# Paged attention of a decoder step: page loads two pages at a time, two low parts on other engines, products over three bank pairs

## The chip, the core and the metric

The kernel runs on one core of one Trainium2 chip. The metric is the device time of one execution in microseconds. The engines in the text: PE is TensorE, DVE is VectorE, ACT is ScalarE, POOL is GpSimd, and SP (SPq in rows) is the sync engine, which here computes nothing: it reads page numbers into registers and issues DMAs. Each engine runs its own instructions in program order; semaphores tie the engines together.

## What is computed

One layer of a hybrid decoder: a half SwiGLU block, one input projection, a convolution branch and a latent attention branch, a gated merge, and a second half SwiGLU block, for 512 prompt tokens and 8 sequences of 8 sample tokens. The change touches only the attention of the 8 sample sequences. Each has 2048 past positions, in 16 pages of 128 rows that a page table names:

```
def one_seq(args):
    q_s, ckv_new, kpe_new, pages = args
    ckv = concat([cache_ckv[pages].reshape(past, 256), ckv_new])
    kpe = concat([cache_kpe[pages].reshape(past, 32), kpe_new])
    k = rmsnorm([einsum('lc,chd->lhd', ckv, w_uk) | kpe], k_head_norm)
    s = einsum('qhd,khd->hqk', q_s, k) * SCALE        # masked
    p = softmax(s)
    return einsum('qhc,chd->qhd', einsum('hqk,kc->qhc', p, ckv), w_uv)
```

Products of full precision are made of three cheaper ones: each operand is split into a high part (a rounded copy) and a low part (the operand minus its high part), and high*high, low*high and high*low are summed.

## The kernel before

Every engine has one hand-written program; the order in it is the order of the work. The sample attention is a stage of 8 sequences (s = 0 to 7) of 16 pages (t), taken in 8 pairs of pages (pp). `sequences` gives the frame on each engine: s = 0 alone, a hardware loop of two sequences a turn, and the last three written out; SP has s = 0 and 1 alone and then its own loop of three turns over s = 2 to 7.

For a pair of pages: SP loads two transposed pages into `c_ring` (8 slots, so four pairs); ACT rounds them to `cT_hi` (`pages_hi`), DVE subtracts to `cT_lo` (`pages_lo`, line 2466), both two deep. PE multiplies each page with the queries and the key weights (line 1861: 12 products of 288 columns), page t into PSUM banks 2 and 3 or 4 and 5 by turns (`page_banks`). ACT copies the scores to `s_buf` and squares the rest into `sq`; DVE sums the squares to `page_ss`. At every fourth page PE adds the rotary scores from `kpeT`.

The softmax of sequence r runs inside sequence r + 1 (`soft_act`, `soft_dve`, `soft_pe`). It needs `kpe_sq`, which POOL makes from all 16 pages of `c_nat`, the rows of the same pages as they lie (line 964). ACT makes the exponentials `p_two`; POOL makes their low part (line 945) and that of the value rows `c_lo` (line 937), and PE multiplies both in two batches of four pairs, before page 12 and before page 15 (lines 1781, 1782), then sums the denominator (line 1791) and folds (line 1796).

SP's part is `load_pages`, four times a sequence: it reads four page numbers from SBUF into registers (`page_of`, line 726, one TENSOR_LOAD each), and with these registers issues four DMAs to `c_ring` (line 731), four to `kpeT` (line 742) and four to `c_nat` (line 737). Three waits stand before them, for `ct_lo` (the ring's slots are free), `pe_scored` and `pages_used`. Behind the last of these on SP stand the loads of the merge weights `w_rawbuf` (line 618), and ACT's program holds their rounding (`split_hi`, line 461) between pairs 4 and 5 of s = 7.

Of the kernel before, what the change touches and what calls it, by code (L numbers as in the profile page):

```python
# [14 lines left out]
F32 = mybir.dt.float32  # L15
# [5 lines left out]
ds = bass.ds  # L21
# [72 lines left out]
def layer(nc, x_t, cols_in, pages_t, pages_in, pages_k, state_conv, page_table, w, const, out):  # L94

    ctx = ExitStack()
    with ctx:
# [14 lines left out]
        def sem(name):  # L112
            return ctx.enter_context(nc.semaphore(name))
# [197 lines left out]
        split_made = sem("split_made")  # L311
# [14 lines left out]
        nat_in = [[sem(f"nat_in{b}{g}") for g in range(NP // 4)] for b in range(2)]  # L326
        ring_in = [sem(f"ring_in{g}") for g in range(2)]
# [194 lines left out]
        SPLITS = PAIRS + 2  # L522
        HIGHS = PAIRS + 2
        LATE_AT = 11
# [9 lines left out]
        def pair_made(r, j):  # L534

            return r * SPLITS + (EARLY_PAIRS + 1 if j < EARLY_PAIRS else j + 3)

# [10 lines left out]
        PEB = 6  # L548

# [24 lines left out]
        def page_banks(t):  # L574

            return 2 + 2 * (t % 2)
# [19 lines left out]
        def _(sp):  # L596
# [131 lines left out]
            def load_ring(g, found):  # L728

                for u, page in enumerate(found):  # L730
                    sp.dma_start(c_ring[:, (4 * g + u + RING // 2) % RING, :], pages_t[ds(page, 1), :, :].rearrange("a p c -> (a p) c"))\  # L731
                        .then_inc(ring_in[g % 2], 16)

            def load_rows(b, g, found):

                for u, page in enumerate(found):
                    sp.dma_start(c_nat[:, b, 4 * g + u, :], pages_in[ds(page, 1), :, :].rearrange("a p c -> (a p) c")).then_inc(nat_in[b][g], 16)  # L737

            def load_kpe(g, found):

                for u, page in enumerate(found):
                    sp.dma_start(kpeT[u * DR:(u + 1) * DR, g % 2, :], pages_k[ds(page, 1), :, :].rearrange("a d t -> (a d) t")).then_inc(kpe_in[g % 2], 16)  # L742
# [12 lines left out]

            sp.wait_ge(rows_done, 2 * NT + PT_TILES)
            found = [page_of(0, u) for u in range(4)]
            load_ring(0, found)
            load_kpe(0, found)
            sp.wait_ge(prep_q, 1)  # L760
            load_rows(0, 0, found)
            for g in (1, 2):
                load_rows(0, g, [page_of(0, 4 * g + u) for u in range(4)])
            sp.wait_ge(prep_tr, 2)
            sp.wait_ge(uk_split, 1)
            found = [page_of(0, 4 + u) for u in range(4)]
            load_ring(1, found)
            load_kpe(1, found)
            load_rows(0, 3, [page_of(0, 12 + u) for u in range(4)])
            for g in (2, 3):  # L770
                found = [page_of(0, 4 * g + u) for u in range(4)]
                sp.wait_ge(ct_lo, 2 * g - 2)
                load_ring(g, found)
                sp.wait_ge(pe_scored, g - 1)
                load_kpe(g, found)
            sp.wait_ge(prep_mm, 2)
            load_pages(1, 1)
# [38 lines left out]
        def _(pool):  # L816
# [124 lines left out]
            def probabilities_low(r, b, half):  # L941

                t = slice(half * NP // 2, (half + 1) * NP // 2)
                pool.wait_ge(p_done, exp_made(r, half))
                ins = pool.tensor_tensor(p_two[:, t, 1, :], s_buf[:, b, t, :], p_two[:, t, 0, :].bitcast(F32), ALU.subtract)
                if half:
                    ins = pool.tensor_tensor(p_two[0:TS, NP, 1, :], s_buf[0:TS, b, NP, :], p_two[0:TS, NP, 0, :].bitcast(F32), ALU.subtract)
                ins.then_inc(split_made, 1)

            def squares(s, b, uses, prev, nxt):  # L950

                if prev and stacked(s):
                    for j in range(EARLY_PAIRS):
                        split_pair(s - 1, 1 - b, j)
                    for half in range(2):
                        probabilities_low(s - 1, 1 - b, half)
                    for j in range(EARLY_PAIRS, PAIRS):
                        split_pair(s - 1, 1 - b, j)
# [19 lines left out]
        def _(act):  # L978
# [316 lines left out]
            def pages_hi(s, pp):  # L1295

                act.wait_ge(ring_in[pp // 2 % 2], (s * 2 + (pp // 4 + 1)) * 64)
# [30 lines left out]
            def pair_high(r, b, j, uses):  # L1328

                act.wait_ge(nat_in[b][j // 2], uses * 64)  # L1330
                act.wait_ge(pages_used, r * PAIRS + (j + 1))
                act.activation(c_hi[j % EARLY_PAIRS][:, :, 0:KL], c_nat[:, b, 2 * j:2 * j + 2, 0:KL], ACT.Copy).then_inc(p_done, 1)
# [99 lines left out]
        def _(pe):  # L1432
# [333 lines left out]
            def soft_pe(r, b):  # L1766
# [8 lines left out]
                if stacked(r + 1):  # L1775
                    for j in range(PAIRS):
# [51 lines left out]
            def pe_seq(s, b, uses, prev, nxt):  # L1828
                soft = soft_pe(s - 1, 1 - b) if prev else None
                for pp in range(NP // 2):  # L1830
# [5 lines left out]
                    for u in range(2):  # L1836
# [5 lines left out]
                        if not (isinstance(s, int) and s == 0 and t < 2):  # L1842
                            pe.wait_ge(page_sq, s * NP + (t - 1))
# [4 lines left out]
                        if prev and stacked(s):  # L1848
                            for _ in range({12: 4, 15: 4}.get(t, 0)):
                                next(soft)  # L1850
                        cols = slice(SQ * b, SQ * b + KQ)
                        for k in range(2):
                            c = (2 * u + k) * P
                            hi, lo = cT_hi[:, pp % 2, c:c + P], cT_lo[:, pp % 2, c:c + P]
                            if prev and k == 1 and t in ((7, 8, 15) if stacked(s) else (7, 8)):
# [79 lines left out]
        def _(dve):  # L1935
# [527 lines left out]
            def pages_lo(s, pp):  # L2463

                dve.wait_ge(ct_hi, s * PAIRS + (pp + 1))
                dve.tensor_tensor(cT_lo[:, pp % 2, :], ring_pair(pp), cT_hi[:, pp % 2, :].bitcast(F32), ALU.subtract).then_inc(ct_lo, 1)  # L2466

# [17 lines left out]
            pages_lo(0, 0)  # L2485
# [11 lines left out]
            def soft_dve(r, b):  # L2497
# [33 lines left out]
                if stacked(r + 1):  # L2531
                    dve.wait_ge(lat_mm, r + 1)
                    dve.tensor_copy(o_lat[:, :], ps[:, 7, 0:PAGE_COLS]).then_inc(soft_step, 1)
                    dve.wait_ge(p_summed, r + 1)
# [67 lines left out]

            def dve_seq(s, b, uses, prev, nxt):
                soft = soft_dve(s - 1, 1 - b) if prev else None
                taps = iter(range(PER))
                for pp in range(NP // 2):
                    if pp + 1 < NP // 2 or nxt:
                        pages_lo(s, pp + 1)
# [34 lines left out]
                    for u in range(2):  # L2643
# [3 lines left out]
                        if prev and stacked(s) and t == NP - 2:  # L2647
                            next(soft)
# [128 lines left out]
```

## Time and profile before

| | us |
|---|---|
| median of three runs (1536.82 to 1539.36) | 1537.03 |
| the profiled execution | 1533.52 |
| its span, first to last instruction | 1531.5 |
| granted TensorE clock, mean share of full | 0.994 |

The sample stage lies at about 706 to 1018 us of the span; before it are the first half block, the projections and the prompt attention, after it the merge and the second half block. The profile shows for each engine when its instructions ran, what ended each idle stretch, and the chain of work that ended last. Rows of SP have the time of issue of a DMA, not of its transfer.

### The profile page before, as it was taken

The page shows a single profiled execution, that of the slowest core. Times are in us where ns is not written, and L with a number is a line of the kernel's source. Part 1 is how long each engine was busy: PE and PEld are TensorE (multiplying, and loading weights), DVE is VectorE, ACT ScalarE, POOL GpSimd, SP SyncE. Part 2 cuts the span into 40 slices and gives each one's busy share as a digit, 9 for nine tenths or more (in the row PEclk, how much of TensorE's full clock was granted, in tenths as well). Part 3 has the DMA queues.
Part 4 walks back from the last instruction along what each step waited for, and adds up shares of the span by engine and source line. Part 5 has one row for each costly group of instructions (what it writes and reads, how often), then busy time and mean ns, then how long its engine had stood idle before and what let it go on. Part 6 is the DMA issues. An engine that isn't in the chain of part 4 may idle for free.

```text
span 1531.5 us, 31143 instructions
## 1 busy us (share of the span) xinstructions
PE 1491.3 (97%) x10771; PEld 1434.9 (94%) x10771; DVE 1067.9 (70%) x1738; ACT 655.5 (43%) x1215; POOL 454.3 (30%) x463
## 2 busy tenths in 40 slices
PE   8999999999999999999999888999999999999999
PEld 8999999999999999588888888888999999999999
DVE  7999898421269975865888788854759998985000
ACT  6444445322221242464666666642434444445111
POOL 4000002454465744320344333223551000005432
PEclk9999999999999999999999999999999999999999
DMA  6233234222333651003444443432222332332322
GB/s 176 70 103 103 82 97 116 78 83 75 82 83 100 83 116 47 13 4 99 129 127 129 124 125 111 128 106 72 83 83 56 109 97 85 106 92 81 91 77 82
DMA packets 245460, 141.69 MB, mean 93 GB/s; under 512 B 22705, under 2 KB 242290, under 8 KB 245362
## 3 DMA queue, kind: packets, MB, share of 16 engines
q1 hardware_dynamic: 244498, 139.97, 33.1%
q8 instruction: 54, 0.88, 0.2%
q10 hardware_dynamic: 864, 0.48, 0.1%
q14 instruction: 44, 0.36, 0.1%
HBM read 136.82 MB, written 3.58 MB: 92 GB/s over the span
## 4 chain that ended last, share of the span: by engine, by line
PE 52%; issue 24%; SPq 11%; POOL 7%; DVE 3%; ACT 1%; DMA 1%; POOLq 0%; DVEq 0%; ACTq 0%
PE ps L493 28%; PE ps L1522 14%; POOL w_lobuf L468 7%; SPq L726 3%; SPq L731 3%; SPq L742 3%; SPq L737 2%; PE ps L1861 2%; PE ps L1647 1%; PE ps L1701 1%; PE ps L1676 1%; PE ps L479 1%; PE ps L1691 1%; DMA w_rawbuf<-in_ffn_w_gu 1%; DVE cT_lo L2466 1%
## 5 line engine op out<-in xcount | busy, mean ns | idle before, releaser
L468 POOL TENSOR_TENSOR w_lobuf<-w_rawbuf,w_hibuf 128x256 fp32r<-128x256 f32 (+1 forms) x328 | 316.4, 996 | 801.4 <-ACT w_hibuf L461 801.3
L1522 PE MATMUL ps<-xs,w 128*128 128x288 f32 x3192 | 427.7, 296 | 0.8 <-DVE w L1984 0.8
L1522 PEld LDWEIGHTS ps<-xs,w 128*128 128x128 f32 x3192 | 426.8, 188 | 1.5 <-issue 1.5
L461 ACT ACTIVATE w_hibuf<-w_rawbuf 128x1024 fp32r<-128x1024 f32 (+1 forms) x89 | 104.4, 1173 | 353.3 <-PE ps L493 332.9
L2192 DVE SCALAR_TENSOR_TENSOR xT<-ps,xT 128x576 f32<-128x576 f32 x23 | 17.4, 756 | 202.4 <-PE ps L493 202.4
L1984 DVE TENSOR_TENSOR w<-w_raw,w 128x512 fp32r<-128x512 f32 x228 | 154.0, 690 | 0.3 <-ACT w L1029 0.2
L493 PE MATMUL ps<-a_hi,w_lobuf 128*128 128x288 f32 x682 | 147.5, 297 | 0.0
L493 PE MATMUL ps<-a_hi,w_hibuf 128*128 128x288 f32 x682 | 147.2, 296 | 0.0
L493 PE MATMUL ps<-x_hi,w_hibuf 128*128 128x288 f32 x656 | 142.2, 298 | 4.1 <-POOL w_lobuf L468 2.9
L493 PE MATMUL ps<-a_lo,w_hibuf 128*128 128x288 f32 x682 | 145.5, 294 | 0.0
L493 PE MATMUL ps<-x_lo,w_hibuf 128*128 128x288 f32 x656 | 140.8, 296 | 0.0
L493 PE MATMUL ps<-x_hi,w_lobuf 128*128 128x288 f32 x656 | 140.7, 296 | 0.0
L1029 ACT ACTIVATE w<-w_raw 128x512 fp32r<-128x512 f32 x228 | 132.2, 624 | 5.7 <-DVE w_raw L1978 2.4
L1861 PE MATMUL ps<-kq_hi,cT_hi 128*128 128x288 f32 x512 | 119.6, 316 | 14.7 <-DVE cT_lo L2466 9.3
L2215 DVE SCALAR_TENSOR_TENSOR y<-ext,cols,y 128x512 f32<-128x512 f32 x120 | 110.6, 922 | 4.1 <-DVE y L2215 1.4
L1861 PE MATMUL ps<-kq_hi,cT_lo 128*128 128x288 f32 x512 | 111.3, 299 | 0.0
L1861 PE MATMUL ps<-kq_lo,cT_hi 128*128 128x288 f32 x512 | 111.3, 299 | 0.0
L493 PEld LDWEIGHTS ps<-x_hi,w_hibuf 128*128 128x128 f32 x656 | 105.4, 188 | 5.8 <-POOL w_lobuf L468 4.1
L493 PEld LDWEIGHTS ps<-a_hi,w_hibuf 128*128 128x128 f32 x682 | 110.2, 189 | 0.0
L493 PEld LDWEIGHTS ps<-a_lo,w_hibuf 128*128 128x128 f32 x682 | 109.3, 188 | 0.0
L493 PEld LDWEIGHTS ps<-a_hi,w_lobuf 128*128 128x128 f32 x682 | 109.0, 188 | 0.0
L1861 PEld LDWEIGHTS ps<-kq_hi,cT_hi 128*128 128x128 f32 x512 | 84.1, 194 | 25.3 <-DVE cT_lo L2466 10.4
(335 smaller groups left out, 2602.6 us busy)
## 6 DMA issues: line engine op xcount, KB each, us to landing
w_raw<-in_ffn_w_gu SPq DMA_DIRECT2D x76, 256.0 KB, 2.9
up_rows<-in_ffn_w_gu SPq DMA_DIRECT2D x72, 256.0 KB, 3.2
c_nat<-in_pages_in SPq DMA_DIRECT2D x128, 144.0 KB, 2.2
c_ring<-in_pages_t SPq DMA_DIRECT2D x128, 128.0 KB, 2.1
w_rawbuf<-in_w_in SPq DMA_DIRECT2D x58, 256.0 KB, 3.2
w_rawbuf<-in_ffn_w_down SPq DMA_DIRECT2D x32, 384.0 KB, 4.0
w_rawbuf<-in_ffn_w_down SPq DMA_DIRECT2D x32, 320.0 KB, 3.4
w_rawbuf<-in_ffn_w_gu SPq DMA_DIRECT2D x24, 256.0 KB, 3.4
```

Source lines behind the costliest of these rows:

```text
L461: act.activation(w_hibuf[:, r % HIS, 0:size], w_rawbuf[:, r, 0:size], ACT.Copy).then_inc(w_hi_done, 1)
L468: ins = pool.tensor_tensor(w_lobuf[:, r, part], w_rawbuf[:, r, part], w_hibuf[:, r % HIS, part].bitcast(F32), ALU.subtract)
L493: mm = pe.matmul(ps[0:width, 2 * s + h, 0:HALF], a, b[:, k, h * HALF:(h + 1) * HALF], start=first and i == 0 and j == 0, stop=last and i = ...
L726: return sp.value_load(pages[0:1, ds(s * NP + t, 1)], min_val=0, max_val=pages_t.shape[0] - 1)
L731: sp.dma_start(c_ring[:, (4 * g + u + RING // 2) % RING, :], pages_t[ds(page, 1), :, :].rearrange("a p c -> (a p) c"))\
L737: sp.dma_start(c_nat[:, b, 4 * g + u, :], pages_in[ds(page, 1), :, :].rearrange("a p c -> (a p) c")).then_inc(nat_in[b][g], 16)
L742: sp.dma_start(kpeT[u * DR:(u + 1) * DR, g % 2, :], pages_k[ds(page, 1), :, :].rearrange("a d t -> (a d) t")).then_inc(kpe_in[g % 2], 16)
L1029: act.activation(w7[b][:, slot, 0, :], src, ACT.Copy).then_inc(w7_hi, 1)
L1522: mm = pe.matmul(ps[:, seven_bank(f, slot), 0:HALF], m, xs[:, slot, n, k, :], start=k == 0 and j == 0, stop=k == KH - 1 and j == 2)
L1861: mm = pe.matmul(ps[:, page_banks(t) + half, 0:KQ], a, m[:, half, cols], start=k == 0 and j == 0, stop=k == 1 and j == 2)
L1984: dve.tensor_tensor(w7[b][:, slot, 1, :], w7_raw[b][:, slot, 1, :], w7[b][:, slot, 0, :].bitcast(F32), ALU.subtract).then_inc(w7_lo, 1)
L2215: dve.scalar_tensor_tensor(dst, src, cw, dst, op0=ALU.mult, op1=ALU.add).then_inc(conv_p_step, 1)
```

## The change

Five things change, all in the sample stage.

- **Loads.** SP's `load_pages` (four groups a sequence) becomes `load_pair` (eight). The list of page numbers is no longer shared: ring, rows and rotary keys each call `found` and read their own. The rows of pages 8 to 15 of sequence s - 1 are loaded among the first four ring pairs of s, those of pages 0 to 7 of s among the last four; the last group of rotary keys of s - 1 comes with pair 1 of s. `ring_in` has one semaphore a ring pair, `nat_in` one a buffer, waited for at all 16 pages.
- **Low part of pages** (`pages_lo`): from DVE to POOL, except in s = 0. On POOL `kpe_sq` of s, which waits for all rows of s, stands ahead of pair 1 of s + 1.
- **Low part of probabilities**: from POOL to DVE, at pair 5.
- **Value products**: four pairs before page 11 and four inside page 14 (before: 12 and 15); the denominator before page 15, the fold after it.
- **Banks**: page products over three pairs of banks (2 and 3, 4 and 5, 0 and 1) instead of two.

SP's program, first rows of its loop: before

```order
446 L726 TENSOR_LOAD pages
447 L726 ISA x3
448 L726 TENSOR_LOAD pages
449 L726 ISA x3
450 L726 TENSOR_LOAD pages
451 L726 ISA x3
452 L726 TENSOR_LOAD pages
453 L726 ISA x2
454 L748 ISA
455 L731 ISA [waits ct_lo]
456 L731 DMA c_ring<-in_pages_t 128x256
```

and of the change (line 736 reads a page number, 744 loads the ring, 750 the rows):

```order
504 L736 TENSOR_LOAD pages
505 L736 ISA x2
506 L764 ISA
507 L744 ISA [waits ct_lo]
508 L744 DMA c_ring<-in_pages_t 128x256
509 L744 ISA
510 L744 DMA c_ring<-in_pages_t 128x256
511 L736 ISA
512 L736 TENSOR_LOAD pages
513 L736 ISA x3
514 L736 TENSOR_LOAD pages
515 L736 ISA x2
```

The body of this loop is two sequences. It holds 32 TENSOR_LOADs and 96 DMAs before, and 96 TENSOR_LOADs and 96 DMAs in the change.

POOL's program, from the end of s = 0 into its loop: before

```order
127 L964 TENSOR_TENSOR c_nat<-c_nat 128x16x32 [waits nat_in02,nat_in01,nat_in03,nat_in00,filled]
128 L512 UNCONDITIONAL_BRANCH
129 L512 ISA
130 L937 TENSOR_TENSOR c_lo<-c_nat,c_hi_140 128x2x256 [waits p_done]
131 L936 REGISTER_ALU
132 L937 TENSOR_TENSOR c_lo<-c_nat,c_hi_141 128x2x256 [waits p_done]
```

and of the change:

```order
127 L553 TENSOR_TENSOR cT_lo<-c_ring,cT_hi 128x512 [waits ct_hi,ct_lo,filled]
128 L987 TENSOR_TENSOR c_nat<-c_nat 128x16x32 [waits nat_in0]
129 L512 UNCONDITIONAL_BRANCH
130 L512 ISA
131 L553 TENSOR_TENSOR cT_lo<-c_ring,cT_hi 128x512 [waits ct_hi]
132 L552 REGISTER_ALU
133 L553 TENSOR_TENSOR cT_lo<-c_ring,cT_hi 128x512 [waits ct_hi]
```

The low parts of the ring pairs now stand in POOL's order, pair 0 of the next sequence ahead of the wait for all rows (`nat_in`) and pair 1 behind it.

The diff, cut to what the steps below speak of:

```diff
         def page_banks(t):
-            return 2 + 2 * (t % 2)
+            return 4 if t == NP - 1 else (2, 4, 0)[t % 3]
+
+        def banks_free(t):
+            return {0: -3, 1: 0, 2: -1, NP - 1: NP - 2}.get(t, t - 2)
...
-            def load_pages(s, b, used=None):
-                for g in range(NP // 4):
-                    found = [page_of(s, 4 * g + u) for u in range(4)]
-                    sp.wait_ge(ct_lo, s * PAIRS + (2 * g - 2))
-                    load_ring(g, found)
-                    sp.wait_ge(pe_scored, s * (NP // 4) + (g - 1))
-                    load_kpe(g, found)
-                    if used is not None:
-                        sp.wait_ge(pages_used, used + 2 * (g + 1))
-                    load_rows(b, g, found)
+            def found(s, t0, n):
+                return [page_of(s, t0 + u) for u in range(n)]
...
+            def load_kpe(s, g):
+                four = found(s, 4 * g, 4)
+                if not (isinstance(s, int) and s == 0 and g < 2):
+                    sp.wait_ge(pe_scored, s * (NP // 4) + (g - 1))
+                for u, page in enumerate(four):
+                    sp.dma_start(kpeT[u * DR:(u + 1) * DR, g % 2, :], pages_k[ds(page, 1), :, :].rearrange("a d t -> (a d) t"))\
+                        .then_inc(kpe_in[g % 2], 16)
+
+            def load_pair(s, b, pp, used=None):
+                two = found(s, 2 * pp, 2)
+                sp.wait_ge(ct_lo, s * PAIRS + (pp - 3))
+                load_ring(pp, two)
+                if pp >= PAIRS // 2:
+                    q = pp - PAIRS // 2
+                    two = found(s, 2 * q, 2)
+                    if used is not None:
+                        sp.wait_ge(pages_used, used + (q + 1))
+                    load_rows(b, q, two)
+                elif used is not None:
+                    q = pp + PAIRS // 2
+                    two = found(s - 1, 2 * q, 2)
+                    sp.wait_ge(pages_used, used + (q + 1 - PAIRS))
+                    load_rows(1 - b, q, two)
+                if pp % 2:
+                    load_kpe(s - 1 if pp == 1 else s, 3 if pp == 1 else (pp - 3) // 2)
...
             with sp.Fori(1, NS // 2) as i:
                 for b in range(2):
-                    load_pages(i * 2 + b, b, i * (2 * PAIRS) + (EARLY_PAIRS + PAIRS * (b - 2)))
+                    for pp in range(PAIRS):
+                        load_pair(i * 2 + b, b, pp, i * (2 * PAIRS) + (EARLY_PAIRS + PAIRS * (b - 2)))
+            for q in range(PAIRS // 2, PAIRS):
+                sp.wait_ge(pages_used, EARLY_PAIRS + PAIRS * (NS - 3) + (q + 1))
+                load_rows(1, q, found(NS - 1, 2 * q, 2))
+            load_kpe(NS - 1, 3)
...
             def squares(s, b, uses, prev, nxt):
+                for pp in range(PAIRS):
+                    if later and pp < PAIRS - 1:
+                        pages_lo(pool, s, pp + 1)
+                    if prev and stacked(s):
+                        for j in ((), (), (0, 1), (2, 3), (), (4, 5), (6, 7), ())[pp]:
+                            split_pair(s - 1, 1 - b, j)
...
+                if nxt:
+                    pages_lo(pool, s, PAIRS)
...
-                for g in range(NP // 4):
-                    pool.wait_ge(nat_in[b][g], uses * 64)
+                pool.wait_ge(nat_in[b], uses * (16 * NP))
                 k = c_nat[:, b, :, KL:KL + DR]
                 pool.tensor_tensor(k, k, k, ALU.mult).then_inc(kpe_sq, 1)
...
                         if prev and stacked(s):
-                            for _ in range({12: 4, 15: 4}.get(t, 0)):
+                            for _ in range({11: 4, 15: 1}.get(t, 0)):
                                 next(soft)
...
+                            if prev and stacked(s) and k == 1 and t == 14:
+                                for _ in range(EARLY_PAIRS):
+                                    next(soft)
...
+            def probabilities_low(r, b):
+                for half in range(2):
+                    t = slice(half * NP // 2, (half + 1) * NP // 2)
+                    dve.wait_ge(p_done, exp_made(r, half))
+                    dve.tensor_tensor(p_two[:, t, 1, :], s_buf[:, b, t, :], p_two[:, t, 0, :].bitcast(F32), ALU.subtract)
...
             def dve_seq(s, b, uses, prev, nxt):
-                    if pp + 1 < NP // 2 or nxt:
-                        pages_lo(s, pp + 1)
+                    if isinstance(s, int) and s == 0 and pp + 1 < PAIRS:
+                        pages_lo(dve, s, pp + 1)
+                    if prev and stacked(s) and pp == 5:
+                        probabilities_low(s - 1, 1 - b)
```

## Rows read from the trace of the kernel before

**Rows 1.** The page, part 1: busy time, share of the span, instructions.

```profile
PE 1491.3 (97%) x10771; PEld 1434.9 (94%) x10771; DVE 1067.9 (70%) x1738; ACT 655.5 (43%) x1215; POOL 454.3 (30%) x463
```

**Rows 2.** The chain that ended last by line, cut to 740 to 860 us.

```profile
by line: issue 25.6%; SPq L726 18.4%; SPq L731 18.3%; SPq L742 16.3%; SPq L737 16.0%; DMA c_ring<-in_pages_t 1.9%; DVE cT_lo L2466 0.6%; ACT cT_hi L1300 0.5%; DVE page_ss L2646 0.5%; DVE s_buf L2654 0.3%; SPq L753 0.3%; DVE top L2523 0.2%; 
```

**Rows 3.** SP's timeline: start, us, engine, line, operation, out<-in, count.

```profile
705.76 2.25 SPq L731 DMA_DIRECT2D c_ring<-in_pages_t  x4
...
741.29 1.88 SPq L731 DMA_DIRECT2D c_ring<-in_pages_t  x4
...
763.33 1.91 SPq L737 DMA_DIRECT2D c_nat<-in_pages_in  x4
...
787.07 1.89 SPq L731 DMA_DIRECT2D c_ring<-in_pages_t  x4
789.21 1.85 SPq L742 DMA_DIRECT2D kpeT<-in_pages_k  x4
791.30 1.92 SPq L737 DMA_DIRECT2D c_nat<-in_pages_in  x4
796.07 2.62 SPq L731 DMA_DIRECT2D c_ring<-in_pages_t  x4
...
837.64 1.92 SPq L737 DMA_DIRECT2D c_nat<-in_pages_in  x4
845.27 1.90 SPq L731 DMA_DIRECT2D c_ring<-in_pages_t  x4
...
992.96 2.69 SPq L737 DMA_DIRECT2D c_nat<-in_pages_in  x4
995.91 0.40 SPq L618 DMA_DIRECT2D w_rawbuf<-in_w_conv_out  x1
```

**Rows 4.** Line 726, 738 to 742 us: duration min/median/max, first and last start.

```profile
L726 SPq TENSOR_LOAD <-pages x4: 260/264/273, 738.9 to 740.6; - x4
```

**Rows 5.** Line 726, 784 to 788 us.

```profile
L726 SPq TENSOR_LOAD <-pages x4: 263/266/274, 784.4 to 786.3; - x4
```

**Rows 6.** What SP waited for, 730 to 995 us.

```profile
SPq L742 <- PE ps L1825: 0.5, 1, 0.5
```

**Rows 7.** Who waited: engine, line, for what, us, times, longest; 730 to 995 us.

```profile
PE ps L1861 <- DVE cT_lo L2466: 8.3, 16, 1.5
...
PE ps L1791 <- DVE o_lat L2533: 5.6, 5, 2.1
PE ps L1861 <- ACT sq L1351: 5.1, 7, 1.0
...
PE ps L1781 <- POOL p_two L947: 4.6, 4, 1.2
```

**Rows 8.** Stretches: length, busy time of each engine, granted clock, DMA share.

```profile
732.80:1018.00 285.20, 255.88 (x1767) 236.94 (x1766) 229.71 (x368) 184.10 (x433) 98.27 (x81) 0.98 0.42 123
806.20:845.30 39.10, 35.88 (x258) 33.68 (x257) 33.49 (x54) 26.33 (x64) 15.76 (x13) 1.00 0.41 122
```

**Rows 9.** PE's timeline, one wait in it.

```profile
851.52 0.38 PE L1791 MATMUL ps<-o_lat,fold 128*128 128x1 f32 x2 [2.08 <-DVE o_lat L2533]
```

**Rows 10.** PE busy and granted clock, microsecond by microsecond.

```profile
853.00:854.00 1.00, 1.00 (x6) 0.50 0.00 1
...
855.00:856.00 1.00, 1.00 (x6) 0.50 0.54 163
856.00:857.00 1.00, 1.00 (x9) 0.95 0.55 168
```

**Rows 11.** VectorE's timeline, one low part of a pair.

```profile
786.95 1.31 DVE L2466 TENSOR_TENSOR cT_lo<-c_ring,cT_hi 128x512 fp32r<-128x512 f32 x1
```

**Rows 12.** GpSimd's timeline, low parts of four pairs of value rows.

```profile
784.84 5.66 POOL L937 TENSOR_TENSOR c_lo<-c_nat,c_hi 128x512 fp32r<-128x512 f32 x4 [11.09 <-ACT c_hi L1332]
```

**Rows 13.** ScalarE's timeline near the end of the pages.

```profile
1001.21 1.06 ACT L461 ACTIVATE w_hibuf<-w_rawbuf 128x1024 fp32r<-128x1024 f32 x1 [6.06 <-DMA w_rawbuf<-in_w_conv_out]
```

More of the change, by code:

```diff
@@ L325, in layer @@
         ukT_done = sem("ukT_done")
-        nat_in = [[sem(f"nat_in{b}{g}") for g in range(NP // 4)] for b in range(2)]
-        ring_in = [sem(f"ring_in{g}") for g in range(2)]
+        nat_in = [sem(f"nat_in{b}") for b in range(2)]
+        ring_in = [sem(f"ring_in{j}") for j in range(RING // 2)]
         kpe_in = [sem(f"kpe_in{g}") for g in range(2)]
@@ L534, in pair_made @@
         def pair_made(r, j):
-            return r * SPLITS + (EARLY_PAIRS + 1 if j < EARLY_PAIRS else j + 3)
+            return r * SPLITS + (j + 1)
         def high_made(r, j):
@@ L548, in layer, with pages_lo @@
         PEB = 6
+        def pages_lo(eng, s, pp):
+            eng.wait_ge(ct_hi, s * PAIRS + (pp + 1))
+            eng.tensor_tensor(cT_lo[:, pp % 2, :], ring_pair(pp), cT_hi[:, pp % 2, :].bitcast(F32), ALU.subtract).then_inc(ct_lo, 1)
         LN_MEAN, LN_VAR = (NS - 3, 8), (NS - 2, 10)
@@ L726, in page_of @@
                 return sp.value_load(pages[0:1, ds(s * NP + t, 1)], min_val=0, max_val=pages_t.shape[0] - 1)
[L728 to L737, printed above, removed]
@@ new lines, in load_ring, with load_rows @@
+            def load_ring(pp, two):
+                for u, page in enumerate(two):
+                    sp.dma_start(c_ring[:, (2 * pp + u + RING // 2) % RING, :], pages_t[ds(page, 1), :, :].rearrange("a p c -> (a p) c"))\
+                        .then_inc(ring_in[pp % (RING // 2)], 16)
+            def load_rows(b, pp, two):
+                for u, page in enumerate(two):
+                    sp.dma_start(c_nat[:, b, 2 * pp + u, :], pages_in[ds(page, 1), :, :].rearrange("a p c -> (a p) c")).then_inc(nat_in[b], 16)
@@ L756, in _ @@
             sp.wait_ge(rows_done, 2 * NT + PT_TILES)
-            found = [page_of(0, u) for u in range(4)]
-            load_ring(0, found)
-            load_kpe(0, found)
+            for pp in range(2):
+                load_ring(pp, found(0, 2 * pp, 2))
+            load_kpe(0, 0)
             sp.wait_ge(prep_q, 1)
-            load_rows(0, 0, found)
-            for g in (1, 2):
-                load_rows(0, g, [page_of(0, 4 * g + u) for u in range(4)])
+            for pp in range(6):
+                load_rows(0, pp, found(0, 2 * pp, 2))
@@ L764, in _ @@
             sp.wait_ge(prep_tr, 2)
             sp.wait_ge(uk_split, 1)
[L766 to L775, printed above, removed]
+            for pp in range(2, 4):
+                load_ring(pp, found(0, 2 * pp, 2))
@@ L776, in _ @@
+            load_kpe(0, 1)
+            for pp in range(6, PAIRS):
+                load_rows(0, pp, found(0, 2 * pp, 2))
+            for pp in range(4, PAIRS):
+                two = found(0, 2 * pp, 2)
+                sp.wait_ge(ct_lo, pp - 3)
+                load_ring(pp, two)
+            load_kpe(0, 2)
             sp.wait_ge(prep_mm, 2)
-            load_pages(1, 1)
+            for pp in range(PAIRS):
+                load_pair(1, 1, pp)
             with sp.Fori(1, NS // 2) as i:
                 for b in range(2):
-                    load_pages(i * 2 + b, b, i * (2 * PAIRS) + (EARLY_PAIRS + PAIRS * (b - 2)))
+                    for pp in range(PAIRS):
+                        load_pair(i * 2 + b, b, pp, i * (2 * PAIRS) + (EARLY_PAIRS + PAIRS * (b - 2)))
@@ L939, in split_pair @@
                     .then_inc(split_made, 1)
[L941 to L948, printed above, removed]
-            def squares(s, b, uses, prev, nxt):
[L952 to L958, printed above, removed]
+            def squares(s, b, uses, prev, nxt):
+                later = not (isinstance(s, int) and s == 0)
+                for pp in range(PAIRS):
+                    if later and pp < PAIRS - 1:
[3 more added lines that the diff above has]
+                            split_pair(s - 1, 1 - b, j)
+                if not later:
+                    pool.wait_ge(ct_lo, PAIRS)
+                if nxt:
+                    pages_lo(pool, s, PAIRS)
                 if not nxt:
                     split_lo(pool, n_merge, n_merge % RAWS, KD * P)
-                for g in range(NP // 4):
-                    pool.wait_ge(nat_in[b][g], uses * 64)
+                pool.wait_ge(nat_in[b], uses * (16 * NP))
                 k = c_nat[:, b, :, KL:KL + DR]
@@ L1841, in pe_seq @@
                             pe.wait_ge(q_hi_done, s + 2)
-                        if not (isinstance(s, int) and s == 0 and t < 2):
-                            pe.wait_ge(page_sq, s * NP + (t - 1))
+                        if not (isinstance(s, int) and s == 0 and t < 3):
+                            pe.wait_ge(page_sq, s * NP + banks_free(t))
                         for part in ln_parts(s, t):
```

25 lines of the change are left out of this document (11 added, 14 removed).

## The prediction, made before the change was run

> **What bounds the kernel now.** I read the page's busy times first. PE is busy 97% of the span [rows 1], so only two things can move the time much: the few waits that PE still has, or something that makes PE wait more. The change lies in the sample stage, so I read that stage by itself. From 732.8 to 1018 us PE is busy 255.9 of 285.2 us, and in one sequence 35.9 of 39.1 us [rows 8]: PE idles about 3 us a sequence, 29 in the stage. The list of waits names the releasers [rows 7]: `cT_lo` of DVE 8.3 us, `o_lat` of DVE 5.6, the squares of ACT 5.1, the low probabilities of POOL 4.6. These 23.6 us are what the moved low parts, the third bank pair and the new places of the value products can reach.
>
> Then I ask why these come late, and the chain of waits answers otherwise than the busy times: from 740 to 860 us it runs over SP, 69% on its four lines and 26% "issue" [rows 2]. The timeline of SP shows why [rows 3]. A group of four pages starts at 787.07 and the next at 796.07, 9.0 us later, four groups a sequence: 36.0 us, as much as PE's 35.9 us of work. And SP hardly waits: 0.5 us in 265 us by its own list [rows 6]. Its cycle is its own work: 1.89 + 1.85 + 1.92 us for three times four DMAs, 0.25 and 0.24 between them, and then 2.85 us (793.22 to 796.07) in which it reads four page numbers. SP and PE are level; SP has no slack to give.
>
> **What a page number costs.** One TENSOR_LOAD itself shows 0.27 us, but the first and the fourth start 1.9 us apart [rows 5], so 0.633 us each with the register work around it; 0.95 us of the 2.85 is there with a single one. A group with two numbers takes 2.85 - 2 x 0.633 = 1.58 us. In straight code without the loop's registers the four starts span 1.7 us [rows 4] and the gap is 2.4 us (738.9 to 741.29): 0.567 each, 1.27 us for two. Two DMAs I take at 0.90 us, near half of 1.89.
>
> The Trainium skill, page "DMA: Bandwidth & Descriptors", section "Latency and other measured facts", gives `tensor_load` a floor of some 600 ns that unrolling by four is to spread. The loop here has them four in a row, and 0.633 us each is what is left: the trace bears the floor out and not the spreading.
>
> **The change, part by part.**
>
> Loads. A sequence has 8 ring groups and 8 row groups of two pages, and 4 rotary groups of four, each with page numbers of its own: 48 numbers where there were 16, for the same 48 DMAs. SP's work: 16 x (1.58 + 0.90) = 39.7 us, and 4 x (2.85 + 1.85) = 18.8 us, together 58.5 us against 36.0. So 22.5 us more a sequence, on the engine that already sets the pace. The six sequences of the loop: 6 x 22.5 = **135.0 us**.
>
> Start. Before, SP came out of its wait for `uk_split` at 705.76 - 2.4 = 703.4 us and ended s = 1 at 763.33 + 1.91 = 765.24 [rows 3]. The change has from there, in straight code, 2 ring pairs, a rotary group, 2 row pairs, 4 ring pairs and a rotary group: 8 x 2.17 + 2 x 4.25 = 25.9 us. Then s = 1 with 12 groups of two and 4 of four, 12 x 2.17 + 4 x 4.25 = 43.0 us, to 772.3: **+7.0 us**. Its waits for `ct_lo` and `pe_scored` should be met by then.
>
> End. Behind the loop come four row groups and a rotary group of s = 7, 4 x 2.17 + 4.25 = **12.9 us**, and only behind them the merge weights, for which ACT waits between pairs 4 and 5 of s = 7. Before they were issued at 995.91, and ACT went on at 1001.21 after 6.06 us of waiting [rows 3, 13]; what follows this moment, the last three pairs, merge and second half block, I leave as it is.
>
> Slack. From 765.24 to 995.65 (992.96 + 2.69) SP took 230.4 us. Six times 36.0 is 216.0; two back edges of the loop cost 2.9 each (839.56 to 845.27 instead of 2.85) [rows 3], some 6; 8.4 us are left, short waits and DMAs that were slow to issue. The waits go, since the others now wait for SP, the slow issues stay. I take half: **-4.2 us**. The back edges stay.
>
> Everything else. The low part of a pair costs 0.7 to 1.3 us on DVE beside POOL's work [rows 11] and 5.66 / 4 = 1.4 us on POOL [rows 12]; once, for the last pairs behind the merge weights, that is on the path: **+0.6 us**. Elsewhere it, the low probabilities on DVE, the third bank pair and the moved value products lie in the shadow of SP: I cost them at nothing, gains too. The cover is about 58.5 - 39.1 = 19 us a sequence; if it were gone, POOL's eight low parts would cost up to 8 x 0.7 = 5.6 us a sequence, and the 23.6 us of waits would be there to win.
>
> New waits, and who stands behind them. Rows 8 to 15 of s now arrive with ring pair 3 of s + 1. POOL waits for all rows before `kpe_sq`, and behind that wait stands `cT_lo` of pair 1 of s + 1; DVE waits for `kpe_sq` at pair 0, and behind it stand its sums of squares, without which ACT stops at page 2. PE likewise waits at page 15 for rotary keys that come with pair 1 of s + 1. So each sequence has a dead stretch in which SP loads four pairs and PE has one to do. Does that hold up SP too? From the moment the rows are in, POOL needs 1.4 us a pair and PE some 3.3; SP asks for pair 1's `cT_lo` only at ring pair 5 of s + 1, a rotary group (4.7), ring 4 with its rows (5.0) and two numbers (1.6) later, 11 us. POOL is done by then. PE has 15 pages, 33 us of work, to place in 58.5 us between arrivals. SP doesn't wait, and its 58.5 us stand.
>
> **The sum.** 7.0 + 135.0 + 12.9 - 4.2 + 0.6 = 151.3 us. The profiled execution took 1533.5 us: 1684.8, say **1685 us**. The median of before lies 3.5 us above that execution; I leave this out, it is well inside the range.
>
> **Rivals.**
>
> *PE's clock.* After an idle stretch of 2.08 us [rows 9] the granted clock fell from 1.00 to 0.50, that is from 2.4 to 1.2 GHz, a microsecond or two later and was back at 0.95 at 856, after some 3.5 us at the low level with PE busy [rows 10]. The change gives PE several longer stretches of idling a sequence. Four or five such drops cost half of 3.5 us each, some 8 us on 36: hidden under 58.5. If the clock stayed at 0.50 for the whole stage, PE's work would be 72 us a sequence, 13.3 over SP's: 1685 + 6 x 13.3 = 1765. It decides from a mean clock of 0.61. Chance 0.05.
>
> *SP waits after all.* If the chain POOL, DVE, ACT behind the late rows takes over 11 us instead of 3 to 6, SP stops at ring pair 5. Every 5 us of that cost 30: 1715. Chance 0.06.
>
> *The floor is one for a batch.* If page numbers cost by the batch and not each, a group would cost 0.95 us whatever its size: SP 16 x 1.85 + 4 x 2.80 = 40.8 us a sequence, against the 38.4 it took (230.4 / 6): 14 us in six, 10 behind the loop, 4 at its start: 1562. The four starts 1.9 us apart speak against it. Chance 0.02. It is what the skill's section named above would say if its spreading held.
>
> *Faster.* If SP in truth had slack, because the page numbers are read while its DMAs would be waiting anyway, the 23.6 us of PE's waits go: 1510. That needs a cycle of SP under PE's 36 us, which with 48 numbers means less than 0.16 us each: the DMAs take 16 x 0.90 + 4 x 1.85 = 21.8 us, what is left of a gap beside its numbers 20 x 0.32 (0.95 - 0.633), and 7.8 us remain for 48. The starts say 0.633, and SP's list of waits is all but empty. Nor can the compiler have merged them: 96 loads stand in the built loop. Chance 0.03.
>
> **How the numbers follow.** The forecast has 0.83. Its own range: low, page numbers at 0.567 in the loop too (32 x 0.066 x 6 = 12.7 less) and all slack gone (4.2 less), 1668; high, 0.71 a number (2.85 / 4: 15 more), and slow issues that grow with the time (8.4 x 58.5 / 36 = 13.6 instead of 4.2: 9 more), 1709. Two DMAs at 0.86 or 0.94 make 4 us either way. With the half of the rival in which SP waits, and leaving the clock, the batch and the fast case out: 1662 to 1718. What a measurement of this kernel can tell from no change is about 0.2%, 3 us. Faster by more 0.03; within 0.01; slower 0.96.
>
> **What would show it.** In the profile of the change: SP's page-number rows three times as many, first and last start of a rotary group of four 1.9 us apart; ring pair 0 of one sequence to that of the next 58 us apart; the merge weights issued near 1147 us of the span; ACT waiting long for `c_ring`, PE's idle time in the stage near 180 us instead of 29, under `cT_lo`, and one wait of 10 us or more a sequence at the rotary keys or the squares; `o_lat` and `p_two` gone from PE's list. The prediction is wrong if SP's list of waits is long (rival two), if the mean clock of the stage is under 0.61 (rival one), or if page numbers start closer than 0.6 us.

## The result

| | us | ratio to before, 95% interval |
|---|---|---|
| before, median | 1536.92 | |
| the change, median of four (1665.82 to 1671.85) | 1671.35 | 1.0866 [1.0838, 1.0894] |
| the change, profiled execution / its span | 1671.85 / 1669.8 | |

The change is 134 us slower. The page's busy times, to be held against [rows 1]:

```profile
PE 1537.1 (92%) x10771; PEld 1478.9 (89%) x10771; DVE 1048.1 (63%) x1700; ACT 657.7 (39%) x1215; POOL 507.2 (30%) x501
```

PE has as many instructions as before, yet 46 us more of busy time. One row of stretches, with the columns of [rows 8], shows both halves of the loss, from ring pair 0 of s = 1 to the end of the stage:

```profile
732.80:1154.00 421.20, 301.95 (x1781) 282.19 (x1780) 210.28 (x329) 187.23 (x436) 149.09 (x118) 0.83 0.29 83
```

The stretch is 136 us longer than that of before. PE idles 119 us in it instead of 29, and its busy time is 302 us instead of 256 at a mean granted clock of 0.83 instead of 0.98: the clock falls in or behind the idle stretches, as to 0.50 from 851 to 854 us behind 1.85 us of standing, and part of the work is done at the low level.

Who sets the pace is seen in the chain of waits, cut to 740 to 1130 us:

```profile
by line: SPq L736 38.5%; issue 25.1%; SPq L750 12.3%; SPq L744 11.8%; SPq L758 11.2%; SPq L764 0.4%; SPq L775 0.2%; SPq L770 0.2%; SPq L756 0.2%; SPq L802 0.1%
```

No computing engine is left in it, and line 736, the reading of page numbers, has twice the share of line 726 in [rows 2]. SP's timeline (start, us, engine, line) shows the cycle:

```profile
775.22 2.20 SPq L758 DMA_DIRECT2D kpeT<-in_pages_k  x4
779.10 0.89 SPq L744 DMA_DIRECT2D c_ring<-in_pages_t  x2
...
833.03 1.86 SPq L758 DMA_DIRECT2D kpeT<-in_pages_k  x4
836.50 0.89 SPq L744 DMA_DIRECT2D c_ring<-in_pages_t  x2
838.77 0.86 SPq L750 DMA_DIRECT2D c_nat<-in_pages_in  x2
841.20 0.86 SPq L744 DMA_DIRECT2D c_ring<-in_pages_t  x2
843.79 0.87 SPq L750 DMA_DIRECT2D c_nat<-in_pages_in  x2
847.12 1.85 SPq L758 DMA_DIRECT2D kpeT<-in_pages_k  x4
850.54 0.90 SPq L744 DMA_DIRECT2D c_ring<-in_pages_t  x2
...
1120.41 1.86 SPq L758 DMA_DIRECT2D kpeT<-in_pages_k  x4
1123.77 7.42 SPq L750 DMA_DIRECT2D c_nat<-in_pages_in  x8
1133.60 1.84 SPq L758 DMA_DIRECT2D kpeT<-in_pages_k  x4
1135.55 0.41 SPq L628 DMA_DIRECT2D w_rawbuf<-in_w_conv_out  x1
```

SP's loop begins at 779.10 and its second sequence at 836.50, 57.4 us later. Its list of waits is empty from 730 to 1140 us. Everyone else waits, as the list of waits of the same stretch says:

```profile
POOL c_nat L987 <- DMA c_nat<-in_pages_in: 88.3, 6, 16.5
DVE kpe_ss L2527 <- POOL c_nat L987: 55.3, 6, 10.1
PE ps L1888 <- POOL cT_lo L553: 47.9, 13, 8.9
...
PE ps L1849 <- DMA kpeT<-in_pages_k: 37.0, 14, 5.0
...
PE ps L1805 <- ACT sq L1374: 11.9, 3, 4.3
...
PE ps L1805 <- DVE p_two L2632: 10.3, 3, 4.1
```

The first four are the dead stretches of the prediction. The last two were not foreseen: line 1805 is the value products, and together they wait 22 us.

Last, the cost of a number, in the view of [rows 5]: a group of four rotary keys in the change, and beside it a line of the kernel before that [rows 5] leaves out.

```profile
L736 SPq TENSOR_LOAD <-pages x4: 263/264/273, 844.7 to 846.4; - x4
L736 SPq FUSED_REGOPS  x4: 147/151/157, 845.0 to 846.7; - x4
```

```profile
L726 SPq FUSED_REGOPS  x8: 46/104/155, 784.3 to 786.6; - x8
```

### The profile page after: what moved, and what is told of

It reads as the page before. It is cut to its first block, busy times and chain, and to the rows that moved or that the text cites. A ratio compares the mean times of both kernels' runs of the same rounds, so it can differ in the third digit from the quotient of the medians.

```text
span 1669.8 us, 31935 instructions
## 1 busy us (share of the span) xinstructions
PE 1537.1 (92%) x10771; PEld 1478.9 (89%) x10771; DVE 1048.1 (63%) x1700; ACT 657.7 (39%) x1215; POOL 507.2 (30%) x501
## 4 chain that ended last, share of the span: by engine, by line
PE 45%; issue 25%; SPq 20%; POOL 6%; DVE 1%; DMA 1%; ACT 1%; POOLq 0%; ACTq 0%
PE ps L493 26%; PE ps L1545 12%; SPq L736 10%; POOL w_lobuf L468 6%; SPq L750 3%; SPq L744 3%; SPq L758 3%; PE ps L1670 1%; PE ps L1699 1%; PE ps L1724 1%; PE ps L479 1%; DMA w_rawbuf<-in_ffn_w_gu 1%; PE ps L1676 1%; PE ps L1681 0%; PE ps L1826 0%
## 5 line engine op out<-in xcount | busy, mean ns | idle before, releaser
L1888 PE MATMUL ps<-kq_hi,cT_hi 128*128 128x288 f32 x512 | 135.9, 351 | 59.4 <-POOL cT_lo L553 58.4
L1888 PEld LDWEIGHTS ps<-kq_hi,cT_hi 128*128 128x128 f32 x512 | 98.1, 222 | 67.0 <-POOL cT_lo L553 36.1
L2679 DVE TENSOR_REDUCE page_ss<-sq 128x8 f32<-128x512 f32 x128 | 84.5, 676 | 105.7 <-ACT sq L1374 105.4
L553 POOL TENSOR_TENSOR cT_lo<-c_ring,cT_hi 128x512 fp32r<-128x512 f32 x56 | 76.8, 1371 | 171.6 <-ACT cT_hi L1323 171.6
L1888 PE MATMUL ps<-kq_hi,cT_lo 128*128 128x288 f32 x512 | 123.3, 326 | 0.0
L1888 PE MATMUL ps<-kq_lo,cT_hi 128*128 128x288 f32 x512 | 121.1, 321 | 0.0
```

Source lines behind the costliest of these rows:

```text
L553: eng.tensor_tensor(cT_lo[:, pp % 2, :], ring_pair(pp), cT_hi[:, pp % 2, :].bitcast(F32), ALU.subtract).then_inc(ct_lo, 1)
L2679: dve.tensor_reduce(page_ss[:, t, :], sq[:, u, 0:H * DN].rearrange("p (h d) -> p h d", d=DN), AX, ALU.add).then_inc(page_red, 1)
```

## The experiments

Four groups of runs; each ratio is to the kernel before on the same chip. e1 to e4 ran on one chip, e5 to e8 on a second, m1 to m3 on a third and m4 on a fourth, so a difference across chips is given by the ratios too.

### Is it the page numbers?

**e2_more_numbers**: the kernel before with 48 numbers a sequence.

```diff
+                    for _ in range(2):
+                        found = [page_of(s, 4 * g + u) for u in range(4)]
                     found = [page_of(s, 4 * g + u) for u in range(4)]
```

> The kernel before, in which SP reads each group's four page numbers three times (48 numbers a sequence for s = 1 to 7) and uses the last reading; nothing else is changed. Theory: 32 more numbers at 0.57 to 0.63 us each for seven sequences, 128 to 141 us less the few us of slack: 1655 to 1672, with four fifths or more of the change's loss in this alone. Rival, the late rows and the wait for them cost the most: under 1600.

Measured: 1655.66 us, ratio 1.0773 [1.0753, 1.0793]; 119 us, 88% of the change's loss, from this edit alone. It adds 224 page numbers; the change adds 244. Its SP timeline:

```profile
783.61 1.92 SPq L737 DMA_DIRECT2D c_nat<-in_pages_in  x4
792.89 1.88 SPq L731 DMA_DIRECT2D c_ring<-in_pages_t  x4
795.03 1.83 SPq L742 DMA_DIRECT2D kpeT<-in_pages_k  x4
797.13 1.91 SPq L737 DMA_DIRECT2D c_nat<-in_pages_in  x4
806.53 1.90 SPq L731 DMA_DIRECT2D c_ring<-in_pages_t  x4
```

The gap between rows and ring is 7.4 us with twelve numbers against 2.85 with four: 0.57 us for each one added. Low end of what was expected, and the rival (late rows cost most) is out.

**e1_shared**: the change with each number read once. The rows then come with their own ring pair and are no longer late.

```diff
             def load_pair(s, b, pp, used=None):
                 two = found(s, 2 * pp, 2)
                 sp.wait_ge(ct_lo, s * PAIRS + (pp - 3))
                 load_ring(pp, two)
-                if pp >= PAIRS // 2:
...
+                if used is not None:
+                    sp.wait_ge(pages_used, used + (pp + 1))
+                load_rows(b, pp, two)
+                if pp % 2:
+                    load_kpe(s, pp // 2, last[0] + two)
+                last[0] = two
```

> The change with each page number read once: a ring pair, the rows of the same pair and, at every second pair, the rotary keys use the same registers; 16 numbers and 48 DMAs a sequence, all else of the change kept (the rows are no longer late, as a consequence). Theory, SP's page numbers are the whole cost: SP's cycle is 8 x 1.57 us for two numbers plus the 48 DMAs and their gaps, about 37 us a sequence, level with PE; time 1515 to 1540. Rival, the low parts on GpSimd and the other moves cost by themselves: over 1570.

Measured: 1557.0 us, ratio 1.0125 [1.0106, 1.0144]. 114 of the 134 us are gone, but 20 stay, more than the theory allows and less than the rival wants.

### What is level with what

**e3_fixed_before** and **e4_fixed_after**: the kernel before, and the change, without the page table.

```diff
             def page_of(s, t):
-                return sp.value_load(pages[0:1, ds(s * NP + t, 1)], min_val=0, max_val=pages_t.shape[0] - 1)
+                return s * NP + t
```

> The kernel before without the page table: page t of sequence s is page 16 s + t of the pool, so SP reads no numbers (the outputs of the sample group are those of other pages). SP's cycle falls to about 26 us, under PE's 36. Theory, SP and PE are level in the kernel before: the waits on c_ring and most of those on cT_lo go, 5 to 18 us less: 1516 to 1529. Rival, SP set nothing before and only the doubled work of the change made it a bound: within 2 us of 1535.

Measured: 1526.68 us, 0.9938 [0.9923, 0.9953], inside the expected range. SP now waits 62 us for `pe_scored` in the stage, where [rows 6] has 0.5:

```profile
SPq L742 <- PE ps L1825: 61.6, 25, 7.2
```

SP did set part of the pace before. But the four waits of PE in [rows 7] stand nearly as they were: 8.1 us for `cT_lo`, 3.9 for `o_lat`, 5.2 for the squares and 4.4 for `p_two`, 21.6 instead of 23.6. SP was not what made these late.

> The change without the page table, as in e3_fixed_before: no numbers, but the late rows, the low parts on GpSimd, the third bank pair and the moved value products stay. Theory, page numbers are the whole loss: 1505 to 1525, below e3_fixed_before by what the other four parts bring (up to 15 us). Rival, the late rows hold POOL and DVE at each sequence's start whatever SP costs: 1550 or more.

Measured: 1554.05 us, 1.0109 [1.009, 1.0129]. The theory missed: with no numbers at all to read the change is 27 us above e3_fixed_before. The time is the rival's, its mechanism is not: POOL's wait for the late rows is down to 1.9 us in the stage. What is there instead stands in PE's timeline, at the first value products of a sequence:

```profile
847.26 0.42 PE L1888 MATMUL ps<-kq_lo,cT_hi 128*128 128x288 f32 x2
851.74 0.38 PE L1805 MATMUL ps<-c_hi,p_two 128*128 128x258 f32 x1 [4.06 <-DVE p_two L2632]
```

in that of ACT,

```profile
845.20 1.28 ACT L1342 ACT_TABLE_LOAD   x1
846.50 0.63 ACT L1342 ACTIVATE p_two<-s_buf 128x512 fp32r<-128x512 f32 x1
...
849.32 0.24 ACT L1347 ACTIVATE s_buf<-s_buf 64x64 f32<-64x64 f32 x1
```

in that of DVE,

```profile
848.88 1.41 DVE L2631 TENSOR_TENSOR p_two<-s_buf,p_two 128x512 fp32r<-128x512 f32 x2
850.21 1.29 DVE L2632 TENSOR_TENSOR p_two<-s_buf,p_two 64x64 fp32r<-64x64 f32 x1
```

and in PE's granted clock (length, busy, clock), microsecond by microsecond:

```profile
852.00:853.00 1.00, 1.00 (x7) 0.61 0.17 46
853.00:854.00 1.00, 1.00 (x7) 0.50 0.72 217
854.00:855.00 1.00, 1.00 (x7) 0.50 0.86 245
855.00:856.00 1.00, 1.00 (x7) 0.68 0.20 70
```

The products stand a page earlier in PE's order, but ACT makes the exponentials where it always did, behind pages 8 and 9, and is done at 849.6; DVE then needs until 851.5 for the low parts. PE stands for 4.06 us, and its clock is between 0.50 and 0.68 for four microseconds with PE busy. Over the six sequences of the stage PE waits 23.0 us at line 1805, against 6.0 at the same products (line 1781) in e3_fixed_before.

In each of these waits two moved parts meet. The last low part on DVE, of 64x64, takes 1.29 us while POOL subtracts a ring pair:

```profile
850.16 1.26 POOL L553 TENSOR_TENSOR cT_lo<-c_ring,cT_hi 128x512 fp32r<-128x512 f32 x1 [4.47 <-ACT cT_hi L1323]
```

In m2_e6_one_read below, where POOL has no ring pairs, the same operation takes 0.21 us, so about 1.1 us of each wait goes with this meeting.

### Which of the other parts

**e5_values_12**: e1_shared with the first value products back before page 12. **e8_after_values_12**: the same edit in the change itself.

```diff
-        LATE_AT = 10
+        LATE_AT = 11
...
-                            for _ in range({11: 4, 15: 1}.get(t, 0)):
+                            for _ in range({12: 4, 15: 1}.get(t, 0)):
```

> e1_shared with the first four value products back before page 12 (and the later high parts after pages 11 and 12); the second four stay inside page 14. Theory: before page 11 PE stands some 4 us a sequence for the low probabilities, because the exponentials are made after page 9's copy whatever the place, and its clock drops for some 3 us behind that; six sequences of 4 + 1.6 us are worth 20 to 34 us: 1523 to 1537. Rival, the low parts on GpSimd are what makes e1_shared slower than the kernel before: 1550 or more.

Measured: 1541.37 us, 1.0033 [1.0018, 1.0048]: above the expected range, but 15.6 us below e1_shared by the medians and 14 by the ratios. The place of four products costs most of what e1_shared had left over; 5 us are still there.

> The change, with its 48 page numbers a sequence, and with the first value products back before page 12, the edit of e5_values_12. Theory, SP's cycle of 57 us hides the place of the products: within 3 us of the change, 1668 to 1675. Rival, the wait for the low probabilities adds to SP's cycle: 1650 or less.

Measured: 1667.18 us, 1.086 [1.0829, 1.089]. The ratio is that of the change within its interval; the median is 4 us lower, 0.8 beyond the bound set. The same edit that is worth 14 to 16 us where SP keeps up is worth 1 us by the ratios and 4 by the medians where it doesn't.

**e6_low_on_dve**: e5_values_12 with the ring pairs' low parts on DVE again.

```diff
-                    if later and pp < PAIRS - 1:
-                        pages_lo(pool, s, pp + 1)
...
-                    if isinstance(s, int) and s == 0 and pp + 1 < PAIRS:
+                    if pp + 1 < PAIRS or nxt:
                         pages_lo(dve, s, pp + 1)
```

> e5_values_12 with the low parts of the ring pairs back on VectorE. What remains of the change is the low probabilities on VectorE, the third bank pair, the second value products inside page 14 and the loads by pairs with shared numbers. Theory: GpSimd takes 1.3 us a pair against 0.7 to 1.3 on VectorE, and PE's wait for them at pair 2 is about 1.3 us a sequence: 0 to 10 us below e5_values_12. Rival, VectorE gains from being rid of them: e6 is 3 us or more above e5.

Measured: 1541.86 us, 1.0038 [1.0022, 1.0054]: no difference to e5, so neither the expected gain nor the rival's loss is seen. The engine of the low parts doesn't show here.

**e7_banks_only**: the kernel before with three bank pairs (`page_banks` and `banks_free` of the change).

> The kernel before with page products over three pairs of banks and nothing else. It can win what PE waits for ACT's squares, 5.1 us in the stage by the trace of before, if SP lets it. Theory, SP is level with PE: 0 to 5 us less, 1532 to 1537. Rival, SP had slack and the whole of 5.1 or more comes: under 1531.

Measured: 1538.88 us, 1.0017 [1.0003, 1.0032]. Not even the 0 to 5 us: the third bank pair alone gains nothing while SP is level with PE. It was not tried alone with SP relieved.

### With SP out of the way, in a kernel that computes all

Reading several page numbers with one instruction relieves SP and keeps the table.

**m1_one_read** is the kernel before with this, from s = 1 on:

```diff
+            def found4(s, g):
+
+                _, values = nc.values_load_multi_w_load_instructions(
+                    pages[0:1, ds(s * NP + 4 * g, 4)], engines=[mybir.EngineType.SP], min_val=0, max_val=pages_t.shape[0] - 1, bass_reorder=False)
+                return list(values)
...
-                    found = [page_of(s, 4 * g + u) for u in range(4)]
+                    found = found4(s, g)
```

> The kernel before, but from s = 1 on the four page numbers of a group are read with one instruction into four registers. If the price is one of the instruction (0.633 us each), SP's gap falls from 2.85 to about 1.3 us a group (the register work and the bounds of four numbers stay) and its cycle from 36 to 30 us: most of what e3_fixed_before brought, 1524 to 1531. If it is one of each number, nothing: 1535 to 1539.

Measured: 1526.57 us, 0.9931 [0.9917, 0.9945]. Faster than both kernels, by as much as having no numbers at all. SP's timeline:

```profile
791.12 1.92 SPq L743 DMA_DIRECT2D c_nat<-in_pages_in  x4
794.76 1.89 SPq L737 DMA_DIRECT2D c_ring<-in_pages_t  x4
796.90 1.84 SPq L748 DMA_DIRECT2D kpeT<-in_pages_k  x4
```

The gap is 1.72 us instead of 2.85, and SP now waits 23.8 us for `pe_scored` in the stage. There is one load in the gap:

```profile
L730 SPq TENSOR_LOAD <-pages x1: 307/307/307, 793.2 to 793.2; - x1
```

The time came as expected, the gap not: about 1.3 us was expected if the whole price were one of the instruction. So only part of it is, 1.13 us for three loads and the three register operations that go with them.

**m2_e6_one_read** and **m3_e5_one_read** are e6 and e5 with the two numbers of a pair read at once.

> e6_low_on_dve (loads by pairs with shared numbers, low probabilities on VectorE, third bank pair, second value products inside page 14) with the two numbers of a pair read by one instruction. With SP no longer level with PE the third bank pair and the products inside page 14 can show: 1518 to 1530, below m1_one_read. Rival, they bring nothing: within 2 us of m1_one_read or above it.

Measured: 1538.09 us, 1.0008 [0.9996, 1.002]; missed, 11.5 us above m1, as the rival had it. PE's longest wait there, and the same one in m1:

```profile
PE ps L1794 <- DVE p_two L2621: 15.8, 6, 3.1
```

```profile
PE ps L1787 <- POOL p_two L953: 4.4, 4, 1.1
```

The total at m1's line is 5.9 us, since 1.5 more are put down to `cT_lo`. The profiled execution of m2 took 1533.98 us, the fastest of twelve, so its waits are not those of the median.

> e5_values_12 (as m2_e6_one_read, but with the low parts of the ring pairs on GpSimd) with the two numbers of a pair read by one instruction. Against m2_e6_one_read it weighs the engine of the low parts with SP out of the way: 1520 to 1535, 0 to 8 us above m2 since GpSimd takes 1.3 us for a pair. Rival, VectorE's relief wins: below m2.

Measured: 1531.62 us, 0.9966 [0.9954, 0.9978]. In the expected range, but below m2: here the rival was right. With SP away it does help that DVE is rid of the ring's low parts; PE's wait for `p_two` is 11.5 us instead of 15.8.

Is the low part of the probabilities later on DVE than on POOL? The last exponential, the last low part and the first value product of one sequence, in m1,

```profile
838.45 0.24 ACT L1327 ACTIVATE p_two<-s_buf 64x64 fp32r<-64x64 f32 x1
840.67 0.77 POOL L953 TENSOR_TENSOR p_two<-s_buf,p_two 64x64 fp32r<-64x64 f32 x1
841.49 0.38 PE L1787 MATMUL ps<-c_hi,p_two 128*128 128x258 f32 x1 [1.10 <-POOL p_two L953]
```

in m2,

```profile
840.55 0.25 ACT L1333 ACTIVATE p_two<-s_buf 64x64 fp32r<-64x64 f32 x1
842.02 0.69 DVE L553 TENSOR_TENSOR cT_lo<-c_ring,cT_hi 128x512 fp32r<-128x512 f32 x1 [1.15 <-ACT cT_hi L1312]
843.83 0.21 DVE L2621 TENSOR_TENSOR p_two<-s_buf,p_two 64x64 fp32r<-64x64 f32 x1
844.28 0.39 PE L1794 MATMUL ps<-c_hi,p_two 128*128 128x258 f32 x1 [2.75 <-DVE p_two L2621]
```

and in m3:

```profile
841.28 0.25 ACT L1339 ACTIVATE p_two<-s_buf 64x64 fp32r<-64x64 f32 x1
842.83 1.30 DVE L2627 TENSOR_TENSOR p_two<-s_buf,p_two 64x64 fp32r<-64x64 f32 x1
844.39 0.38 PE L1800 MATMUL ps<-c_hi,p_two 128*128 128x258 f32 x1 [2.06 <-DVE p_two L2627]
```

From the end of the exponential to the end of the low part it takes 2.75 us on POOL in m1, 3.24 in m2, where DVE does a ring pair first, and 2.60 in m3. So in m3 the low part is no later than in m1. PE waits longer because it is ready sooner, 0.8 us behind the exponential instead of 1.7. What puts it ahead, the third bank pair or something else, was not tried.

**m4_values_14** is m1 with the second value products inside page 14 and the denominator before page 15.

```diff
-                            for _ in range({12: 4, 15: 4}.get(t, 0)):
+                            for _ in range({12: 4, 15: 1}.get(t, 0)):
...
+                            if prev and stacked(s) and k == 1 and t == 14:
+                                for _ in range(EARLY_PAIRS):
+                                    next(soft)
```

> m1_one_read with the second four value products inside page 14 instead of before page 15, the denominator before page 15 and the fold behind it; low probabilities and everything else as in m1. Theory: m2 and m3 lose because the low probabilities queue on VectorE (15.8 and 11.5 us of PE's waits), not by this move, which takes away PE's 3.9 us for o_lat: 1519 to 1526. Rival, the products inside page 14 are themselves what costs in m2: 1530 or more.

Measured: 1525.25 us, 0.9942 [0.9925, 0.9958]. In the expected range and as fast as m1; the ratios can't part them, so neither a gain nor a small loss from the move is shown. A loss of the size that m2 has, and with it the rival, is out.

## Why the prediction was right, and where it was wrong

**The forecast held**: 1671 for 1685, inside 1662 to 1718, by the cause that was named. Term by term, from the timeline of SP:

- *Loop.* Forecast 230.4 + 135.0 - 4.2 = 361 us. Measured from 777.42 (775.22 + 2.20) to 1122.27 (1120.41 + 1.86), 344.9 us. This is the mis-sized term, by 16 us, and two errors are in it. I priced all 48 numbers at 0.633 us. The ring's groups cost that: 1.57 us for two (839.63 to 841.20). But most gaps before two rows are 1.38 us (837.39 to 838.77), and those before four rotary keys about 2.46 (844.66 to 847.12), which is 0.57 a number, with one register operation to a number in place of two. I had this value as my low end. By these gaps a sequence needs 54.9 us and not 58.5, about 22 us less in six. The other error goes the other way: some 10 us of slow issues stayed in the loop, where I kept 4.2.
- *Start.* Forecast +7.0 us, SP through s = 1 at 772.3. Measured 777.4, 5 us later. This offsets a third of the loop's error, and that part of the close number is luck.
- *End.* Forecast 12.9 us behind the loop, measured 13.2 (1122.27 to 1135.44).
- *Merge weights.* Forecast near 1147 us, measured 1135.55: 139.6 us after those of [rows 3], the sum of the terms above. From there to the end of the span it takes 534.3 us, before 535.6: what follows was rightly left as it is.

**The signs were mixed.** Those on SP held: it waits for nothing, its period is 57.4 us for 58, and PE has dead stretches under `cT_lo` and at the rotary keys. Others failed. The first and last load of a rotary group of four start 1.7 us apart in most groups, not 1.9; I had named numbers closer than 0.6 us as a sign that the prediction is wrong, and in that price, for most of the rows and rotary keys, it was. ACT's list has no wait for `c_ring`; ACT waits for PE's pages. PE's longest wait is 8.9 us, not 10. `p_two` did not leave PE's list, but grew from 4.6 to 10.3 us. PE's idle time in the stage is 119 us and not 180; the other 46 us of the longer stage are PE busy at the low clock. These are 6.6 us for each of seven sequences, near the 8 of my rival, and I had counted them as hidden. As time they were: PE had the room.

**The step that failed is the one on everything else**, costed "at nothing, gains too", with the words that without SP's cover "the 23.6 us of waits would be there to win". This was right for the sum, as SP covered it (e8_after_values_12), and wrong for what lies under it. With SP relieved the other parts together don't gain, they cost: 27 us from e3_fixed_before to e4_fixed_after. I had looked at which waits the moved products would end and not at what they themselves wait for; ACT's exponentials stood in the same timeline, after page 9. 14 to 16 us of it are the first products' place (e5_values_12). How the rest divides stays open. PE waits longer for `p_two` in m2 and m3 than in m1, but m3's rows show that the low probabilities on DVE are not late there; neither they nor the third bank pair was tried alone with SP relieved. My price for the low parts of the ring pairs on POOL, up to 5.6 us a sequence without SP's cover, was wrong too: m3, which has them on POOL, is 6.5 us faster than m2.

**The rivals.** *Faster* was refuted in both halves: SP had no slack (e3_fixed_before, m1_one_read), and with slack the change would still be slower than before. *The floor is one for a batch* fell for single reads: 0.57 us for each number added in e2. The Trainium skill ("DMA: Bandwidth & Descriptors", "Latency and other measured facts") has a floor of some 600 ns for `tensor_load`, which unrolling is to amortize; the price here is near that floor, and twelve loads in a row did not spread it. *SP waits after all*: it had no wait. *The clock*: the mean of 0.83 lies above the 0.61 from which it would decide.

## What to carry to other kernels

An engine that only reads registers and issues DMAs has no busy time on the page, yet it can be level with the busiest engine: take the distance between two like DMA groups in its own timeline and hold it against the period of the loop before giving it work. A value read into a register has a price, and part of it is one of the instruction; read neighbours with one instruction and use them for all transfers that need them. Count the register operations around each load as well as the loads. Before moving an instruction forward in an engine's order, ask what its operands wait for; if they are not made earlier too, it waits in front of work that was ready.

## What the runs showed of the hardware that was not expected

- One TENSOR_LOAD of four registers and its four bounds checks make a gap of 1.72 us on SP; four single ones make 2.85.
- A page number costs 0.57 us where one register operation goes with its load and 0.633 us where two do: four numbers with 4 operations start 1.7 us apart in the change, four with 8 operations 1.9 us apart in the kernel before. The load itself shows 0.26 to 0.27 us in both. No run changed the register operations alone.
- A 64x64 subtraction on DVE took 1.29 to 1.30 us beside a subtraction on POOL (e4_fixed_after, m3_e5_one_read) and 0.21 us where POOL had none (m2_e6_one_read).
- After PE stood for 4.06 us in e4_fixed_after, the granted clock was 0.61, 0.50, 0.50 and 0.68 in four successive microseconds in which PE was busy throughout, 1.7 us lost.
